# Banded attention in a two-block transformer kernel: GpSimd takes a quarter of the softmax's division, and two output products are begun later

## What is computed

```
k_sh, v_sh = split(rmsnorm(h, kv_norm) @ w_kv)          # 4 key/value heads of 64
q = partial_rotary((rmsnorm(h, b_pre_norm) @ b_w_q).reshape(512, 16, 64))
scores = q_block . [previous block, own block] keys / 8  # 128 x 256 a head, banded mask
probs = softmax([scores, sink])[..., :-1]
attn = (probs @ v) @ b_w_o
```

## Time and profile before

| | |
|---|---|
| median of 3 runs | 1810.18 us (1809.99 to 1810.55) |
| span of the profiled execution | 1808.7 us |
| TensorE busy | 1759.7 us, 97% of the span |
| VectorE, ScalarE, GpSimd busy | 64%, 46%, 44% |
| attention units, from the first score to the rest of the output product | 1318.96 to 1411.32 us |
| granted TensorE clock | 1.00 in every stretch of this stage |

### The profile page before, as it was taken

How to read it: one execution, slowest core, us unless ns; L and a number is a source line. 1 busy time by engine, 2 the same in 40 slices (tenths; PEclk the granted TensorE clock), 3 DMA queues, 4 the chain that set the end, 5 groups by cost and what they waited for, 6 DMA issues and landing times.

```text
span 1808.7 us, 30009 instructions
## 1 busy us (share of the span) xinstructions
PE 1759.7 (97%) x10632; PEld 1541.6 (85%) x10632; DVE 1150.7 (64%) x2034; ACT 832.0 (46%) x1399; POOL 803.9 (44%) x975
## 2 busy tenths in 40 slices
PE   6999999999999999999999999999999999999998
PEld 5778888878788878899899999888966799999886
DVE  6784776476766763888588777412658388777312
ACT  3423331365556552555365555423556465555322
POOL 0365455330101151766456666463423166666461
PEclk9999999999999999999999999999999999999999
DMA  9543565321111233134314343322321124343321
GB/s 324 179 141 93 151 186 192 105 78 39 55 58 52 70 128 116 47 94 139 115 49 117 93 116 116 128 93 93 104 76 47 47 71 117 93 116 93 128 93 70
DMA packets 212888, 191.12 MB, mean 106 GB/s; under 512 B 10443, under 2 KB 192578, under 8 KB 212802
## 3 DMA queue, kind: packets, MB, share of 16 engines
q1 hardware_dynamic: 212160, 189.69, 33.6%
q10 hardware_dynamic: 642, 0.29, 0.1%
HBM read 187.86 MB, written 2.10 MB: 105 GB/s over the span
## 4 chain that ended last, share of the span: by engine, by line
PE 64%; issue 15%; POOL 8%; DVE 7%; ACT 4%; DMA 1%; SPq 0%; POOLq 0%; DVEq 0%; ACTq 0%
PE PS L2265 21%; PE PS L2266 20%; PE PS L2267 20%; POOL slot_low L718 3%; POOL w_low L735 2%; POOL w_low L749 2%; ACT w_high L858 1%; PE PS L2395 1%; POOL gate_sum_a L702 1%; DMA x<-in_x 1%; POOL h_sum_low L708 1%; DMA w_raw<-in_o_w_out 1%; DVE masked L2207 0%; PE PS L2983 0%; DVE ada_part L1417 0%
## 5 line engine op out<-in xcount | busy, mean ns | idle before, releaser
L735 POOL TENSOR_TENSOR w_low<-w_raw,w_high 128x256 fp32r<-128x256 f32 x465 | 378.7, 849 | 476.2 <-ACT w_high L858 450.5
L718 POOL TENSOR_TENSOR slot_low<-w_raw,slot_high 128x256 fp32r<-128x256 f32 x400 | 319.1, 824 | 176.4 <-ACT slot_high L1217 173.7
L858 ACT ACTIVATE w_high<-w_raw 128x2048 fp32r<-128x2048 f32 (+3 forms) x90 | 165.2, 1836 | 326.9 <-PE PS L2267 293.4
L2265 PE MATMUL PS<-h_high,w_high 128*128 128x512 f32 (+1 forms) x688 | 248.6, 361 | 6.2 <-POOLq L753 1.7
L2266 PE MATMUL PS<-h_low,w_high 128*128 128x512 f32 (+1 forms) x688 | 241.2, 351 | 0.0
L2267 PE MATMUL PS<-h_high,w_low 128*128 128x512 f32 (+1 forms) x688 | 241.1, 350 | 0.0
L2265 PE MATMUL PS<-h_sum_high,slot_high 128*128 128x256 f32 x800 | 227.2, 284 | 4.7 <-DVE joined L2021 3.9
L2267 PE MATMUL PS<-h_sum_high,slot_low 128*128 128x256 f32 x800 | 226.4, 283 | 0.0
L2266 PE MATMUL PS<-h_sum_low,slot_high 128*128 128x256 f32 x800 | 226.4, 283 | 0.0
L2265 PE MATMUL PS<-h_high,slot_high 128*128 128x256 f32 x600 | 170.1, 284 | 1.9 <-ACT PS L1231 1.9
L2266 PE MATMUL PS<-h_low,slot_high 128*128 128x256 f32 x600 | 169.8, 283 | 0.0
(11 more groups left out here) (386 smaller groups left out, 4059.4 us busy)
## 6 DMA issues: line engine op xcount, KB each, us to landing
w_raw<-in_f_gate_up SPq DMA_DIRECT2D x88, 512.0 KB, 5.0
w_raw<-in_f_down SPq DMA_DIRECT2D x40, 512.0 KB, 4.0
w_raw<-in_e_w_in SPq DMA_DIRECT2D x32, 512.0 KB, 5.1
gains<-in_ada_w SPq DMA_DIRECT2D x16, 1024.0 KB, 5.3
w_raw<-in_a_w_in SPq DMA_DIRECT2D x24, 512.0 KB, 5.1
w_raw<-in_o_w_in SPq DMA_DIRECT2D x20, 512.0 KB, 4.3
ada_raw<-in_ada_w SPq DMA_DIRECT2D x8, 1024.0 KB, 12.7
w_raw<-in_e_w_out SPq DMA_DIRECT2D x16, 512.0 KB, 6.3
```

The lines of the kernel that those rows point to most:

```text
L718: ins = nc.gpsimd.tensor_tensor(slotL[j][:, piece], src[:, piece], slotH[j][:, piece].bitcast(F32), ALU.subtract)
L735: ins = nc.gpsimd.tensor_tensor(WL[s][:, piece], raw[s][:, piece], WH[s][:, piece].bitcast(F32), ALU.subtract)
L858: nact(WH[s][:, 0:n], raw[s][:, 0:n], ACT.Copy).then_inc(w_high[s], 1)
L2265: mm(dst, lh, rh, start=first, stop=False, skip_group_check=True)
```

## The change

1. **GpSimd normalises the fourth head** of every unit from unit 2 on (`POOL_FROM`). VectorE's reciprocal raises a new semaphore `r2_ready`; VectorE multiplies three heads and GpSimd the fourth, 128 x 256 (or 128 x 128), in place. TensorE waits for it (`p2_pool`) ahead of the fourth head's transposes.
2. **GpSimd's low parts are cut into slices between the units**: for the last query chunk 2, 3 and 3 instructions ahead of its normalisation in units 2, 3 and 4, for the first two chunks of `w_o` two instructions ahead of each of the units 6 to 9 and 10 to 13.
3. **The products begun ahead** are one in each of the last four units: `kt` 0 and 1 move from unit 9 to units 12 and 13.
4. The three semaphores of the keys' rotation become one that counts; no instruction changes by it.

```diff
+POOL_FROM = 2
...
+            def normalise(n):
+
+                w = 0 if n % T else P
+                pool.wait_ge(r2_ready, n + 1)
+                last = p2[n % 2][:, GROUP - 1, w:2 * P]
+                nc.gpsimd.tensor_scalar(last, last, soft[:, n % 2, 7, GROUP - 1:GROUP], None, ALU.mult).then_inc(p2_pool, 1)
...
                     low(0, 0)
                     low(0, 1)
                     low(1, 0)
-                    low(1, 1)
+                    for of, s, j, units in (("q", 1, 1, (2, 3, 4)), ("wo", 0, 0, (6, 7, 8, 9)), ("wo", 1, 0, (10, 11, 12, 13))):
+                        done = 0
+                        for n in units:
+                            count = BASE[of].split[s] + j + 1
+                            pool.wait_ge(w_high[s], count)
+                            upto = CHUNK * (n - units[0] + 1) // len(units) // SLICE * SLICE
+                            for c in range(done, upto, SLICE):
+                                piece = slice(c, c + SLICE)
+                                ins = nc.gpsimd.tensor_tensor(WL[s][:, piece], raw[s][:, piece], WH[s][:, piece].bitcast(F32), ALU.subtract)
+                            done = upto
+                            if done == CHUNK:
+                                ins.then_inc(w_split[s], 1)
+                            normalise(n)
+                        pool.wait_ge(w_split[s], count)
+                        pool.sem_inc(raw_free[s], 1)
+                        if of == "q":
+                            normalise(5)
+                    for n in range(14, UNITS):
+                        normalise(n)
                     continue
...
                 if name == "wo":
                     first = 1
-                    low(0, 0)
-                    low(0, 1)
...
-                steps.link(v.reciprocal(st[:, 7, :], st[:, 5, :]))
-                pr = p2[n % 2][:, :, w:2 * P]
-                v.tensor_tensor(pr, pr, st[:, 7, :].unsqueeze(2).broadcast_to((P, GROUP, 2 * P - w)), ALU.mult).then_inc(p2_ready, 1)
+                v.reciprocal(st[:, 7, :], st[:, 5, :]).then_inc(r2_ready, 1)
+                dve.wait_ge(r2_ready, n + 1)
+                heads = GROUP if n < POOL_FROM else GROUP - 1
+                pr = p2[n % 2][:, 0:heads, w:2 * P]
+                v.tensor_tensor(pr, pr, st[:, 7, 0:heads].unsqueeze(2).broadcast_to((P, heads, 2 * P - w)), ALU.mult).then_inc(p2_ready, 1)
...
                 for h in range(GROUP):
+                    if h == GROUP - 1 and n >= POOL_FROM:
+                        pe.wait_ge(p2_pool, n - POOL_FROM + 1)
                     for k in range(0 if n % T else 1, 2):
...
-            AHEAD = {UNITS - 2: (2, 3), UNITS - 1: (3, 4)}
+            AHEAD = {UNITS - 4: (0, 1), UNITS - 3: (1, 2), UNITS - 2: (2, 3), UNITS - 1: (3, 4)}
...
-                if n == UNITS - 7:
-                    ahead_wo(0, 2)
```

More of the change, by code:

```diff
@@ L404, in program @@
         oh_ready, ol_ready, q2_half = sem("oh_ready"), sem("ol_ready"), sem("q2_half")
-        k2_raw, k2_turn, k2_rot, kd_ready, v2_ready = (sem(n) for n in ("k2_raw", "k2_turn", "k2_rot", "kd_ready", "v2_ready"))
+        k2_step, kd_ready, v2_ready = (sem(n) for n in ("k2_step", "kd_ready", "v2_ready"))
         q2_raw, q2_turn, q2_ready, q2_sin, q2_cos = (sem(n) for n in ("q2_raw_ready", "q2_turn", "q2_ready", "q2_sin", "q2_cos"))
@@ L413, in program @@
             sem(n) for n in ("half_sum", "hs_ready", "hs_act", "hs_dve", "hs_pool"))
-        s2_read = sem("score2_read")
+        s2_read, r2_ready, p2_pool = sem("score2_read"), sem("r2_ready"), sem("p2_pool")
+        K2_RAW, K2_TURN, K2_ROT = 1, 2, 3
         out_done = sem("out_done")
@@ L1323, in _ @@
             act.wait_ge(used[1], end_use("kv", 1))
-            nact(q2raw[:, :, :], PS[:, 2:4, :], ACT.Copy).then_inc(k2_raw, 1)
+            nact(q2raw[:, :, :], PS[:, 2:4, :], ACT.Copy).then_inc(k2_step, 1)
             split_high("kv", 1, 1)
@@ L1327, in _ @@
                 high_tile(TR["q"], t, 2 * t)
-            act.wait_ge(k2_rot, 1)
+            act.wait_ge(k2_step, K2_ROT)
             for g in range(KVH):
@@ L2172, in _, with rotate @@
             sin2 = sinB.unsqueeze(1).broadcast_to((P, 2, S))
-            def rotate(dst, bank, raw_ready, copies, turned):
+            def rotate(dst, bank, raw_ready, copies, turned, turns):
                 dve.wait_ge(raw_ready, copies)
                 v.tensor_tensor(dst[:, :, :], q2raw[:, :, :], cos2, ALU.mult)
-                dve.wait_ge(turned, 1)
+                dve.wait_ge(turned, turns)
                 steps.link(v.tensor_tensor(q2tmp[:, :, :], PS[:, bank:bank + 2, :], sin2, ALU.mult))
@@ L2184, in _ @@
             low_tile(q, 1, 6)
-            rotate(q2[1], 2, k2_raw, 1, k2_turn).then_inc(k2_rot, 1)
+            rotate(q2[1], 2, k2_step, K2_RAW, k2_step, K2_TURN).then_inc(k2_step, 1)
             low_tile(q, 2, 4)
@@ L2229, in _ @@
             steps.link(v.tensor_scalar(minus_sinks[:, :], sinks[:, :], -1.0, None, ALU.mult))
-            rotate(q2[0], 6, q2_raw, 2, q2_turn).then_inc(q2_ready, 1)
+            rotate(q2[0], 6, q2_raw, 2, q2_turn, 1).then_inc(q2_ready, 1)
             top2(0)
@@ L2915, in _ @@
             turn_queries(3)
-            pe.wait_ge(k2_raw, 1)
+            pe.wait_ge(k2_step, K2_RAW)
             pe.wait_ge(late_in, 48)
@@ L2919, in _ @@
                 ins = mm(PS[:, 2 + m, :], turn_b, q2raw[:, m, :], start=True, stop=True)
-            ins.then_inc(k2_turn, 1)
+            ins.then_inc(k2_step, 1)
             B = BASE["q"]
```

## The result

The changed kernel takes 1824.01 us (median of 5, 1821.54 to 1824.51) against 1810.18 us: 13.8 us slower. The ratio is 1.0071, 95% interval 1.006 to 1.0082. The forecast was 1815.4 us with a range up to 1818.9: the direction came out, the size did not.

A forecast was written before the change was run, and what follows sets the result against it. TensorE was taken to bound units up to 7, VectorE's chain units 9 to 13. Waits of 3.2 (unit 2) and 2.0 (unit 6) plus 0.0 (units 9 to 15) gave +5.2 us on 1810.18: 1815.4 us, range 1812.6 to 1818.9.

The forecast's parts named there:

- The clock was 1.00 in both halves and enters no term.: TensorE's clock in both halves of the attention, read as 1.00 before the change and given no cost in the forecast.
- Taking them away there gains nothing.: The two products behind unit 9 were hidden by a 1.53 us wait; in units 12 and 13 they add 2.94 us.
- units 9 to 15: 0.0: Net term for units 9 to 15: moved products against an earlier start, 0.0 us, bounds 1.3 worse and 1.5 better.
- the earlier start: Unit 14's scores start 1.5 us earlier, through shorter VectorE multiplications (0.9 at most) and fewer lock waits (some 0.5).
- The two waits: TensorE waits for GpSimd's head behind two slices: +3.2 us in unit 2, +2.0 us in unit 6.
- The bound of 1.46: Upper cost in us of GpSimd's normalisation, its slowest form of this size; with it the sum is +8.7 us.
- The lock: VectorE and GpSimd each wait until the other's instruction has ended; where GpSimd is free, TensorE's wait costs nothing.
- The extra instruction ahead of the first TENSOR_SCALAR: Rival: on GpSimd between slices and unit 2's normalisation, its length adds to 1815.4 us, about 1821 us; chance 0.10.
- Faster: VectorE is the path in every unit: Rival: 14 units save about 0.27 us each, 1806.4 us; chance 0.06.
- The added waits don't bind: Rival: ScalarE makes the chunk's high part earlier, so GpSimd's head is ready in time, 1810.2 us; chance 0.05.
- The end gives back more: Rival: VectorE gains 1.5 to 2 us at the stage's end, a short normalisation leaves 4.5 before: 1812.7 us; chance 0.15.
- The loads: Slices end later, so loads such as that of the second half of `w_o` start later; cost nothing.

The follow-up runs named there:

- f4: The changed kernel with 24 transposes of the identity ahead of TensorE's wait in unit 2 and 18 in unit 6: 1818.46 us.
- h2: The changed kernel with identity transposes inside the waits of units 2 and 6 and the two output products back behind unit 9: 1814.45 us.
- f1: The changed kernel with the two output products back behind unit 9: 1818.34 us.
- g1: The changed kernel with GpSimd's heads of units 2 and 6 ahead of the slices and the two products back behind unit 9: 1807.76 us.
- g3: The changed kernel with products behind unit 9, GpSimd taking heads only from unit 8, slices only for unit 9's chunk, bursts for units 1 and 5: 1808.64 us.
- g4: The kernel before with the two products moved from unit 9 to units 12 and 13, and 22 identity transposes in their old place: 1812.26 us.

## Why the prediction was wrong

- **"The clock was 1.00 in both halves and enters no term."** This is the step that failed. It was true of the kernel before and was carried over to a kernel for which I had just worked out two new waits of 2 to 3 us on TensorE. f4 and h2 price it at 4.0 us behind those waits (3.0 in f1's execution). With some 3 more behind unit 9 (windows and remainder, not isolated) it is over half of the stage's 12.15 us.
- **"Taking them away there gains nothing."** As a sentence about gain it held; about cost it was never asked. The products behind unit 9 were hidden, and they were also what kept TensorE busy. The term "units 9 to 15: 0.0" measured +2.4: -1.9 for the heads (forecast -1.5 from the earlier start), +1.3 for the products' work and some 3 us left, which the windows lay to the clock.
- **The two waits** (+3.2 and +2.0) were right in mechanism and near in size: 5.8 us by h2, unit for unit 3.5 and 2.3. GpSimd's head was priced at 0.74 as displayed and takes 0.92 or 0.93 alone; that is 0.4 of the 0.6 missing. The bound of 1.46 was not needed, though where VectorE holds the lock the head shows up to 1.69.
- **The lock** was read rightly, and where GpSimd is free it holds TensorE up nowhere: g1 has no wait of TensorE for GpSimd at all.
- **The rivals.** The extra instruction ahead of the first TENSOR_SCALAR, at 0.10, is refuted by 0.06 us between slice and head; the 6 us that the Trainium skill, "GPSIMD Engine Reference", section "Instruction dispatch", gives for a first call do not occur here. "Faster: VectorE is the path in every unit" is refuted by g3. "The added waits don't bind" is refuted by the waits of 3.35 and 2.56 us. "The end gives back more" had the heads' gain right (1.9 us, where it said 1.5 to 2), but the waits measured 5.8 and not its 4.5. No rival had the clock, so the range missed by 5.1 us.
- **The loads** that start later waited for nobody, as said: no wait of ScalarE or TensorE for a load is new.

## What to carry to other kernels

Price an added TensorE wait like these (2.6 to 3.4 us) twice: once for itself, and once for the slower products behind it, here about 2 us each (2.0 in the changed kernel's profiled execution, 1.5 in f1's). Work that fills a gap is not free to move just because the gap hides it; before moving it, write down what will keep the engine busy instead. When an in-order engine takes on small urgent work between slices of large work, put the urgent item ahead of any slice that waits for a third engine; that order alone is worth 12 us here and turns the change from a loss of 13.8 into, with the products back, a gain of 2.5 us (1807.76 against 1810.28).

## What was unexpected of the hardware

- An idle stretch of 2.56 us, with 0.56 us idle and six transposes ahead of it and an otherwise full stage before that, was followed by products at half rate (1.98 us for eight that take 1.08). One of 1.53 or 1.56 us was not, and one of 1.75 us (g4) was, in the profiled execution.
- The penalty varies between executions of one program, and the mean granted clock with it. f1 read 0.997 at 1816.54 to 1818.34 us and 0.995 at 1819.49 and 1821.19 us; g4 read anything from 0.997 to 0.999.
- Useless transposes inside a wait paid for themselves: 5.6 us by the medians and 4.1 in the stage, for 42 of them.
- GpSimd's one-input multiplication by a per-partition scalar (0.92 us for 128 x 256) is slower than its two-input subtraction of the same size (0.74). VectorE's part in the lock is as the earlier trace rows: a head that issues behind VectorE's 128 x 768 shows 1.68 or 1.69.
- Open: why g4 keeps the clock in some executions and not in others, and how the 4.3 us of the moved products divide exactly, beyond the 1.3 of their work.
